# Gathering the token rows of two experts with one stationary load, turning the first hidden chunk two pieces later, and keeping the scaled result in another tile

## The reference, cut to what matters

```python
def moe_swiglu(h, router_w, w1, w3, w2):     # h: 256 tokens x 1024
    logits = xf @ router_w                    # 8 experts
    top_val, top_idx = lax.top_k(logits, 2)
    gates = jax.nn.softmax(top_val, axis=-1)
    ...
    # for each expert e, for its rows: (silu(x @ w1[e]) * (x @ w3[e])) @ w2[e]
    # w1, w3: 1024 x 3584, w2: 3584 x 1024, float32
    ...
    out = segment_sum(y * gate)               # each row back to its token
```

## Time and profile before

| | |
|---|---|
| median of 3 runs | 1721.47 us (1720.77 to 1722.89) |
| the profiled execution | 1721.34 us |
| its span | 1719.3 us |
| TensorE busy | 97% of the span |
| VectorE, ScalarE busy | 79%, 65% |
| mean granted TensorE clock | 0.991 of 2.4 GHz |
| expert stage | from about 565 us to 1711 us, nine passes |

### The profile page before, as it was taken

The page is one execution under the profiler, slowest core; times in us unless marked ns, Lnnn a source line. Parts: engine busy times, 40 slices in busy tenths (PEclk is TensorE's granted clock), DMA queues, the critical chain, the costliest instruction groups (busy, mean ns, idle before and its releaser), DMA issues.

```text
span 1719.3 us, 20965 instructions
## 1 busy us (share of the span) xinstructions
PE 1665.0 (97%) x8406; PEld 1381.9 (80%) x8406; DVE 1364.3 (79%) x1571; ACT 1114.0 (65%) x1367; POOL 76.4 (4%) x49
## 2 busy tenths in 40 slices
PE   6998999999999999999999999999999999998997
PEld 4865899997688888788788788788888787786885
DVE  2483778895332999998998998998998998997995
ACT  3364444442324787887887887887887887785883
POOL 0000000000000000200200200200101001000000
PEclk9999999999999999999999999999999999999998
DMA  9934687877613699999999999998998998996990
GB/s 353 361 129 170 222 301 264 305 272 290 231 54 147 249 361 340 339 376 344 342 376 345 340 368 352 340 371 340 344 378 333 347 379 313 344 353 244 373 357 27
DMA packets 169712, 518.96 MB, mean 302 GB/s; under 512 B 6765, under 2 KB 8954, under 8 KB 169610
## 3 DMA queue, kind: packets, MB, share of 16 engines
q1 hardware_dynamic: 156704, 473.32, 73.9%
q10 hardware_dynamic: 12906, 44.25, 6.8%
HBM read 516.50 MB, written 1.05 MB: 301 GB/s over the span
## 4 chain that ended last, share of the span: by engine, by line
PE 85%; DVE 8%; ACT 3%; POOL 1%; DMA 1%; issue 1%; ACTq 0%; DVEq 0%; POOLq 0%
PE bank L1094 17%; PE bank L1098 17%; PE bank L1097 17%; PE bank L644 8%; DVE w_lo L1934 5%; PE bank L638 3%; PE bank L829 2%; PE bank L831 2%; PE bank L830 2%; PE bank L1030 2%; PE bank L1108 2%; PE bank L782 2%; POOL rstd L553 1%; PE bank L849 1%; PE bank L850 1%; PE bank L847 1%
## 5 line engine op out<-in xcount | busy, mean ns | idle before, releaser
L1934 DVE TENSOR_TENSOR w_lo<-ring,w_hi 128x1024 fp32r<-128x1024 f32 x756 | 918.5, 1242 | 82.2 <-ACT w_hi L1407 56.4
L1407 ACT ACTIVATE w_hi<-ring 128x1024 fp32r<-128x1024 f32 x756 | 794.9, 1062 | 216.5 <-PE bank L1098 214.5
L1094 PE MATMUL bank<-w_hi,hg_hi 128*128 128x512 f32 x1008 | 396.7, 394 | 3.8 <-DVE w_lo L1934 3.8
L1098 PE MATMUL bank<-w_hi,hg_lo 128*128 128x512 f32 x1008 | 394.1, 391 | 0.0
L1097 PE MATMUL bank<-w_lo,hg_hi 128*128 128x512 f32 x1008 | 393.7, 391 | 0.0
L1094 PEld LDWEIGHTS bank<-w_hi,hg_hi 128*128 128x128 f32 x1008 | 190.1, 189 | 47.1 <-DVE w_lo L1934 7.5
L1098 PEld LDWEIGHTS bank<-w_hi,hg_lo 128*128 128x128 f32 x1008 | 189.8, 188 | 39.8
L1097 PEld LDWEIGHTS bank<-w_lo,hg_hi 128*128 128x128 f32 x1008 | 190.2, 189 | 38.6
L1094 PE MATMUL bank<-w_hi,hid_hi 128*128 128x512 f32 x504 | 199.5, 396 | 0.0
L1098 PE MATMUL bank<-w_hi,hid_lo 128*128 128x512 f32 x504 | 196.8, 390 | 0.0
L1097 PE MATMUL bank<-w_lo,hid_hi 128*128 128x512 f32 x504 | 196.5, 390 | 0.0
(11 more groups left out here) (290 smaller groups left out, 1735.2 us busy)
## 6 DMA issues: line engine op xcount, KB each, us to landing
ring<-in_moe_w SPq DMA_DIRECT2D x168, 2048.0 KB, 8.0
ring<-in_ada_w SPq DMA_DIRECT2D x24, 2048.0 KB, 12.8
ring<-in_moe_w ACTq DMA_DIRECT2D x21, 2048.0 KB, 8.0
ring<-in_ffn_w SPq DMA_DIRECT2D x15, 2048.0 KB, 8.4
ring<-in_da_w_in SPq DMA_DIRECT2D x6, 2048.0 KB, 20.2
ring<-in_gla_w_in SPq DMA_DIRECT2D x6, 2048.0 KB, 13.2
ring<-in_da_w_out SPq DMA_DIRECT2D x2, 2048.0 KB, 8.4
ring<-in_gla_w_out SPq DMA_DIRECT2D x2, 2048.0 KB, 8.5
```

What stands on the lines that cost most here:

```text
L1094: begun = mm(out[:, :], xhi, whi[:, cs], start=first, stop=False)
L1098: last = mm(out[:, :], xlo, whi[:, cs], start=False, stop=end)
L1407: A(w_hi[:, Q % PIECES, :], raw_piece(m, q), ACT.Copy).then_inc(hi_done, 1)
L1934: v.tensor_tensor(w_lo[:, Q % PIECES, :], raw_piece(m, q), w_hi[:, Q % PIECES, :].bitcast(F32), ALU.subtract).then_inc(lo_done, 1)
```

## The change

- **Groups.** Experts are gathered in groups: (0), (1, 2), (3, 4), (5, 6), (7, 8), (9), (10). The gather of a group stands in the pass before its first expert, so in experts 0, 2, 4, 6 and 8. For a group of two, `Pm` of both experts is the moving operand (256 columns), and the result of either part fills the four banks 0, 1, 6 and 7.
- **High and low apart.** As both parts use the same banks, the high part is gathered after piece 76, the low part after piece 79 (`LOW_AT`), and it waits until ScalarE has copied the high part. VectorE's copies stand at q = 80. Each copy (128x512) goes to runs of 128 columns in the halves of both experts; there are four for each part in a group of two.
- **First turn.** Chunk 0 is turned after piece 19 instead of piece 17, and its parts are taken two steps later.
- **Scaled result.** `high_out` and `low_out` write into `hid_hi`, `hid_lo` (the half of even chunks), and `spread` reads there.
- **Slots.** `Pm` has two halves, and VectorE makes both of a group in the pass before. It uses expert 8's number in expert 6, and reads the overflow registers before expert 6 instead of 7. `par` and `tri` share their place with it.

```diff
-    TURN_AT = {g_last["w3", c] + 2: c for c in range(ECH)}
+    TURN_AT = {g_last["w3", c] + (2 if c else 4): c for c in range(ECH)}
+    LOW_AT = GATHER_AT + 3
+    GROUPS = [(0,)] + [(m, m + 1) for m in range(1, NE, 2)] + [(m,) for m in range(NE + 1, NE + OVER)]
+    group_in = {group[0] - 1: g for g, group in enumerate(GROUPS)}
...
-        Pm = sb("Pm", [P, TT, P], F32R)
+        Pm = sb("Pm", [P, TT, 2, P], F32R)
...
+        def gathered_tiles(g, w, n):
+            group = GROUPS[g]
+            if len(group) == 1:
+                return w[:, group[0] % 2, n * 512:(n + 1) * 512]
+            out = w[:, :, :].rearrange("p b (k c) -> p k b c", k=KT)
+            return out[:, 2 * n:2 * n + 2, :, :]
+
+        def gathered_bank(g, n, low):
+            if len(GROUPS[g]) == 1:
+                return psum[(6 if low else 0) + n][:, :]
+            bank = psum[(0, 1, 6, 7)[n]][:, :]
+            return bank.rearrange("p (k b c) -> p k b c", k=2, b=2)
...
-            def gather(m):
-                pe.wait_ge(s_P, m + 1)
-                for h, banks in ((h_hi, (0, 1)), (h_lo, (6, 7))):
-                    if m == 0 and h is h_lo:
-                        pe.wait_ge(s_htl, 4)
-                    for g, bank in enumerate(banks):
-                        for k in range(4):
-                            own = slice((4 * g + k) * P, (4 * g + k + 1) * P)
-                            for tt in range(TT):
-                                last = mm(psum[bank][:, k * P:(k + 1) * P], h[:, tt, own], Pm[:, tt, :],
-                                          start=(tt == 0), stop=(tt == TT - 1))
-                    last.then_inc(s_gt, 1)
+            def gather(g, low):
+                group = GROUPS[g]
+                h, banks = (h_lo if low else h_hi), (0, 1, 6, 7)
+                if len(group) == 1:
+                    banks = (6, 7) if low else (0, 1)
+                pe.wait_ge(s_P, g + 1)
+                if low and g == 0:
+                    pe.wait_ge(s_htl, 4)
+                elif low:
+                    pe.wait_ge(s_gh, g + 1)
+                per = KT // len(banks)
+                n = P * len(group)
+                for k in range(KT):
+                    for tt in range(TT):
+                        slots = Pm[:, tt, :, :] if len(group) == 2 else Pm[:, tt, group[0] % 2, :]
+                        last = mm(psum[banks[k // per]][:, k % per * n:(k % per + 1) * n],
+                                  h[:, tt, k * P:(k + 1) * P], slots, start=(tt == 0), stop=(tt == TT - 1))
+                last.then_inc(s_gt, 1)
...
-                    mm(psum[2 + n][:, :], to, hg_1[0][:, (m - 1) % 2, own], start=True, stop=False)
+                    mm(psum[2 + n][:, :], to, hid_1[0][:, 0, own], start=True, stop=False)
...
-                    if q == GATHER_AT and m + 1 < NE + OVER:
-                        gather(m + 1)
+                    if q == GATHER_AT and m in group_in:
+                        gather(group_in[m], False)
+                    if q == LOW_AT and m in group_in:
+                        gather(group_in[m], True)
...
-            def gathered(m):
-                act.wait_ge(s_gt, 2 * m + 1)
-                for g in range(2):
-                    last = A(hg_1[0][:, m % 2, g * 512:(g + 1) * 512], psum[g][:, :], ACT.Copy)
+            def gathered(g):
+                act.wait_ge(s_gt, 2 * g + 1)
+                for n in range(2 * len(GROUPS[g])):
+                    last = A(gathered_tiles(g, hg_1[0], n), gathered_bank(g, n, False), ACT.Copy)
...
-                    last = A(hg_1[0][:, m % 2, own], y_raw[:, own], ACT.Copy, scale=gcol[:, 0:1])
+                    last = A(hid_1[0][:, 0, own], y_raw[:, own], ACT.Copy, scale=gcol[:, 0:1])
...
-                        e = m + 1 if m + 1 < NE else over[m + 1 - NE]
-                        dispatch(m + 1, e)
-                        gates_of(e)
+                        gates_of(expert_id(m + 1))
+                        for j in GROUPS[group_in[m]] if m in group_in else ():
+                            dispatch(j, expert_id(j))
...
-            for m in range(NE - 1):
+            for m in range(NE - 2):
                 expert(m)
             dve.wait_ge(s_ovf, 1)
             more = [dve.value_load(ovi[0:1, o:o + 1], min_val=1, max_val=2) for o in range(OVER)]
             over = [dve.value_load(ovi[0:1, OVER + o:OVER + o + 1], min_val=0, max_val=NE - 1) for o in range(OVER)]
+            expert(NE - 2, over)
             expert(NE - 1, over)
```

More of the change, by code:

```diff
@@ L451, in raw_piece, with group_of @@
             return ring[:, ring_slot(m, i) % SLOTS, p * SUB:(p + 1) * SUB]
+        def group_of(m):
+            return next(g for g, group in enumerate(GROUPS) if m in group)
+        def gathered_tiles(g, w, n):
[9 more added lines that the diff above has]
+            return bank.rearrange("p (k b c) -> p k b c", k=2, b=2)
         def piece_no(m, q):
@@ L1039, in spread @@
                     to, own = PmT[:, tt * P:(tt + 1) * P], slice(half * 512, (half + 1) * 512)
-                    mm(psum[2 + n][:, :], to, hg_1[0][:, (m - 1) % 2, own], start=True, stop=False)
-                    mm(psum[2 + n][:, :], to, hg_1[1][:, (m - 1) % 2, own], start=False, stop=True).then_inc(s_sct, 1)
+                    mm(psum[2 + n][:, :], to, hid_1[0][:, 0, own], start=True, stop=False)
+                    mm(psum[2 + n][:, :], to, hid_1[1][:, 0, own], start=False, stop=True).then_inc(s_sct, 1)
             def slots_turned(m):
@@ L1046, in slots_turned @@
                 for tt in range(TT):
-                    nc.tensor.transpose(psum[7][:, tt * P:(tt + 1) * P], Pm[:, tt, :].bitcast(F32), ident[:])
+                    nc.tensor.transpose(psum[7][:, tt * P:(tt + 1) * P], Pm[:, tt, m % 2, :].bitcast(F32), ident[:])
                 for tt in range(TT):
-                    last = mm(psum[7][:, S:S + 1], Pm[:, tt, :].bitcast(F32), gsel[:, tt:tt + 1],
+                    last = mm(psum[7][:, S:S + 1], Pm[:, tt, m % 2, :].bitcast(F32), gsel[:, tt:tt + 1],
                               start=(tt == 0), stop=(tt == TT - 1))
@@ L1061, in expert @@
                         if what == "w1" and c == 0:
-                            pe.wait_ge(s_gh, m + 1)
+                            pe.wait_ge(s_gh, group_of(m) + 1)
                         elif what == "w1":
@@ L1126, in _ @@
             pe.wait_ge(s_hth, 4)
-            gather(0)
+            gather(0, False)
+            gather(0, True)
             keep_pace(1, 2)
@@ L1495, in expert @@
                         last.then_inc(s_g2e, 1)
-                    if q == GATHER_AT + 1 and m + 1 < NE + OVER:
-                        gathered(m + 1)
+                    if q == GATHER_AT + 1 and m in group_in:
+                        gathered(group_in[m])
                     if m == NE - 1 and q % PPC == 1 and q // PPC - 1 + SLOTS >= PER:
@@ L1875, in dispatch @@
                 for tt in range(TT):
-                    last = v.tensor_scalar(Pm[:, tt, :], slot_no[:], posx[:, int(m >= NE), tt, own], None, ALU.is_equal)
-                last.then_inc(s_P, 1)
+                    last = v.tensor_scalar(Pm[:, tt, m % 2, :], slot_no[:], posx[:, int(m >= NE), tt, own], None,
+                                           ALU.is_equal)
+                if m == GROUPS[group_of(m)][-1]:
+                    last.then_inc(s_P, 1)
             def gates_of(e):
@@ L1936, in split_to, with gathered @@
                     tiles_done[0] += 1
[L1938 to L1942, removed]
+            def gathered(g):
+                dve.wait_ge(s_gt, 2 * g + 2)
+                for n in range(2 * len(GROUPS[g])):
+                    last = v.tensor_copy(gathered_tiles(g, hg_1[1], n), gathered_bank(g, n, True))
                 last.then_inc(s_gl, 1)
@@ L1957, in low_out, with expert_id @@
                     own = slice(half * 512, (half + 1) * 512)
-                    last = v.scalar_tensor_tensor(hg_1[1][:, m % 2, own], y_raw[:, own], gcol[:, 0:1],
-                                                  hg_1[0][:, m % 2, own].bitcast(F32), ALU.mult, ALU.subtract)
+                    last = v.scalar_tensor_tensor(hid_1[1][:, 0, own], y_raw[:, own], gcol[:, 0:1],
+                                                  hid_1[0][:, 0, own].bitcast(F32), ALU.mult, ALU.subtract)
                 last.then_inc(s_eye, 1)
             def expert(m, over=None):
+                def expert_id(j):
+                    return j if j < NE else over[j - NE]
                 m_end = max(m, NE - 1)
@@ L1998, in expert @@
                         overflow_table()
-                    if q == GATHER_AT + 1 and m + 1 < NE + OVER:
-                        gathered(m + 1)
+                    if q == LOW_AT + 1 and m in group_in:
+                        gathered(group_in[m])
                 if m >= NE - 1:
```

8 lines of the change are left out of this document (4 added, 4 removed).

## The result

The changed kernel took 1702.22 us (median of 4 runs, 1698.21 to 1705.27) against 1721.12 (4 runs, 1719.71 to 1722.89): a ratio of 0.9888, 95% interval 0.9865 to 0.9912. Run again beside the last experiments it took 1700.66 us (4 runs, 1700.15 to 1702.61), ratio 0.9878 (0.9863 to 0.9893). The forecast was 1700.4, the range 1696.5 to 1708.

The account below looks back on a forecast made before the run. TensorE's queue was taken as the bound, with VectorE 10.7 us behind. Terms -12.8 + 0.05 - 9.4 + 1.2 = -21.0 us gave 1700.4 us from a profiled 1721.34, range 1696.5 to 1708 for 8 in 10.

Parts of the forecast that it names:

- Bound: Expert stage: TensorE sets the pace, busy 124.03 of 125.15 us an expert, with VectorE 10.7 us behind it.
- Part 1: Gather on TensorE: one gather for two experts, 256-column matmuls at 0.120 us each, gains 12.8 us.
- Rival C: Gather: 256 columns cost twice 128, so merging gains 0; total 1713.1 us, chance 0.04.
- Part 2: Double gather's copies on ScalarE and VectorE: others don't wait, 1.7 and 2.3 us in hand, cost 0.
- rival E: Gather copies: each 128-column run costs as a whole copy, making the kernel slower; 1746 us, chance 0.04.
- Part 3: First turn of experts 1 to 7, two pieces later: the wait for VectorE's product goes, gain 9.4 us.
- Rival B: First turn: the wait moves to VectorE's difference of piece 20 instead of going; 1709.8 us, chance 0.08.
- Part 4: Scaled result in another tile and Pm twice as wide: same instructions at the same shapes, cost 0.
- Part 5: VectorE's overflow-register reads before expert 6: expert 6 loses 3.1 us, expert 7 1.2 instead of 3.1, net cost 1.2.
- Rival D: Expert stage: DMA can't pass 353 GB/s, experts stay at 125.1 us; about 1720 us, no change, chance 0.03.
- The sign on ScalarE: Expected in the new trace: ScalarE still waits for TensorE, but by about 20 us less.
- The sum: Whole kernel: -12.8 + 0.05 (expert 8's split gather) - 9.4 + 1.2 = -21.0 us.

Follow-up runs that it names:

- the kernel with the turn alone: The kernel before, with only the first turn (chunk 0) moved two pieces later: 1712.45 us, ratio 0.9940.
- the kernel with two small matmuls: The changed kernel, with each 256-column gather matmul issued as two of 128 columns, each with its own load of weights: 1715.31 us, ratio 0.9953.
- spread reads: The changed kernel, with the six register reads one each at pieces 41 to 46 instead of together at an expert's start: 1698.33 us, run again 1698.35 us.
- the kernel with the tile alone: The kernel before, with only the scaled result kept in the hidden tile instead of the gathered one: 1721.72 us, ratio 1.0001.
- the turn taken back: The changed kernel, with the first turn back at two pieces after its w3 instead of four: 1713.04 us, ratio 0.9942.

## Why the prediction was right, point by point

- **Bound.** TensorE's queue was the only one without slack: with some 13 us less work in it and 9 us less lost at the turns, its stretches are 100% busy and VectorE is still 7.7 us below it (112.46 of 120.18). Two readings of the prediction were loose without changing a term: the stretches that agree before are five, not six (125.15 to 125.18), and of the 9.1 us ahead of spreads 0.76 belongs to expert 6's result, not to the last two.
- **Part 1, -12.8 us.** Held, and a little more: 0.120 us for 256 columns (1.92 us for 16), and two neighbouring experts take 244.3 us where the kernel with the turn alone takes 247.6, 3.35 us a pair for 3.2 forecast. Rival C falls by the trace of the changed kernel and by the kernel with two small matmuls, which gives 3.4 us a pair back. The Trainium skill's 134 cycles for 128 columns (TensorE: Matmul & The Clock Gate, Back-to-back issue gap) are there the gap of an isolated matmul, and the same section says that this is too little for a stream of loads and matmuls with few columns, for which it gives some 81 ns. This stream is slower than either: 32 took 3.52 us from start to start, 0.110 each, where the first would make 1.8 and the second 2.6 us (both estimates).
- **Part 2, 0.** Held, with both margins within 0.2 us of the ones worked out. Copies in runs of 128 cost no more than plain ones (602 against 595 ns a copy on ScalarE, 681 against 686 on VectorE), so rival E has no ground. The three pieces between high and low are what keeps it at 0.
- **Part 3, -9.4 us.** Held: 1.34 us in each of seven experts, shown by the kernel with the turn alone and by the one with it taken back. Rival B falls: 1.5 us were in hand at the turn, and no difference became the wait.
- **Part 4, 0.** Held for the tile by its own experiment. Missed in one place: the slots of two experts are now made at once on VectorE (four instructions, 0.87 us instead of 0.47), and in expert 0 the gains of the last scaling follow directly behind. The product of chunk 1 is then late by 0.44 us. VectorE in the kernel before and in the changed one, then the turn:

```profile
603.05 0.47 DVE L1876 TENSOR_SCALAR Pm<-slot_no,posx 128x128 fp32r<-128x128 f32 x2
```

```profile
606.76 0.87 DVE L1911 TENSOR_SCALAR Pm<-slot_no,posx 128x128 fp32r<-128x128 f32 x4
```

```profile
618.39 1.09 PE L1140 MATMUL bank<-ident,work 128*128 128x128 f32 x8 [0.44 <-DVE work L2019]
```

  It is there in every kernel with doubled slots, the one with the old turn too, and in none of those built from before. In the other experts no wait shows at a turn.
- **Part 5, +1.2 us.** The sum was right (1.4), its two terms were off: expert 6 lost 2.7 instead of 3.1, expert 7 1.7 instead of 1.2. VectorE's pause alone is a little shorter (2.78 us, not 3.13, the row below), and at expert 7 a difference some 13 us behind the spread is late as well (0.47 us), a wait that I had counted at expert 6 only.

```profile
1307.44 1.29 DVE L1987 TENSOR_TENSOR ada_acc<-bank,work 128x512 f32<-128x512 f32 x2 [2.78 <-issue]
```

- **Rival D.** Falls: 367 GB/s over a whole pass, no wait of ScalarE for a landing in the expert stage.
- **The sign on ScalarE.** "By about 20 us less" holds for all its waits for TensorE (19.4), but not for those for weight buffers, which the earlier trace rows name: these fell by 9.7. The others are the ones at the first turn and the gather.
- **The sum.** -21.0 forecast; -21.3 from first turn to first turn in the second profile, -19.7 in the first, -18.9 in the medians of the first runs (1702.22 against 1721.12) and -21.2 in those of the later ones (1700.66 against 1721.84). The difference between the two profiles is TensorE's clock, not a step of the working. That the forecast and the later median agree within 0.3 us is in part luck. Part 1 gave 0.6 us more than its term, the late chunk 1 took 0.4 and Part 5 0.2, and the clock of the start moves a total by more than these.

## What to carry to other kernels

When one engine's instruction queue is the bound, price each instruction in it by the distance between starts of the same shape elsewhere in the trace: here that showed matmuls of 128 columns to be nearly as dear as ones of 256 (0.110 and 0.120 us), so that merging two users of the same stationary operand nearly halved their cost. An engine that waits for a product of the neighbour is helped by issuing what is ready first, by as many pieces as the wait is long, and the reserve beyond that buys nothing. The register reads cost time only where they stood in a row directly ahead of a hand-over; spread over pieces with slack they were free.

## What the runs showed of the hardware that was not expected

- The same wait of 4.2 us, followed by the same instructions, gave 129.89 us in one profile, 130.10 to 130.57 in three and 131.24 to 131.29 in three others. TensorE stayed at 1.2 GHz for longer in the slower ones. In the changed kernel's second profile, then in the one with spread reads:

```profile
1551.00:1562.00 11.00, 6.80 (x18) 4.84 (x19) 8.69 (x10) 6.35 (x7) 0.00 (x0) 0.76 0.50 201
```

```profile
1548.00:1559.00 11.00, 6.59 (x15) 4.71 (x16) 8.25 (x10) 5.50 (x7) 0.00 (x0) 0.52 0.53 210
```

- The start of the kernel, to which no edit adds work, differs by up to 5.6 us between profiles: the first turn of expert 0 stood at 588.96 in the kernel with the tile alone, 590.79 before, 594.55 with the turn taken back, and 594.44 in the first profile of the change once its two pieces are taken off. Over the first 60 us the granted clock was 0.97, 0.94, 0.91 and 0.91. Of the thirteen profiles, the nine with the change in them had 0.91 or less there in five, the four built from before in none. Whether the change has a part in that or chance alone is open.
- Six register reads hold VectorE for 2.8 and ScalarE for 2.4 us when issued in a row, while one a piece costs TensorE nothing.
